# A decode step with new places for its small pieces, and a second quarter of the chosen rows loaded by SyncE

## What is computed

```python
rows_full = concat([cache_kv[page_table], rows_new])     # 4096 + 1 rows a request, from pages
kc, vc = compress(rows_full[:, :, 0]), compress(rows_full[:, :, 1])   # 255 compressed rows
o_cmp, p = cmp_attention(q, kc, vc)
sel = top_k(select_blocks(p), 16)                       # 16 blocks of 64 rows, for each group
o_slc = selected_attention(q, blocks(rows_full[:, :, 2]), blocks(rows_full[:, :, 3]), sel)
o_win = window_attention(q, last 512 rows)
o = g0 * o_cmp + g1 * o_slc + g2 * o_win
```

## Time and profile before

| | |
|---|---|
| median of three runs | 2114.49 us (2113.04 to 2121.23) |
| the profiled execution | 2107.58 us, its span 2105.8 us |
| TensorE busy | 1971.9 us (94% of the span) |
| VectorE, ScalarE, GpSimd busy | 882.5, 735.3, 565.1 us |
| mean granted TensorE clock | 0.983 |

### The profile page before, as it was taken

One profiled execution on the slowest core, in us unless ns is written; L12 is line 12 of the kernel. 1 busy time (PEld: TensorE's weight loads), 2 busy tenths in 40 slices (PEclk: granted clock), 3 DMA queues, 4 the chain that ended last, 5 costly groups with the idle time before them and its releaser, 6 DMA issues. The chain is left out here.

```text
span 2105.8 us, 25188 instructions
## 1 busy us (share of the span) xinstructions
PE 1971.9 (94%) x9303; PEld 1356.8 (64%) x9303; DVE 882.5 (42%) x1781; ACT 735.3 (35%) x1345; POOL 565.1 (27%) x585
## 2 busy tenths in 40 slices
PE   8999999999999999999996898888888888899997
PEld 7888888888888887777774454444444444444442
DVE  0354545454531014444445355454554545511127
ACT  0231133213310003223323665666566665510013
POOL 0000000000002003343345476656466565030000
PEclk9999999999999999999998999999999999999999
DMA  5222222222222321111114555547374563563224
GB/s 199 89 80 91 91 71 80 91 91 71 80 82 102 100 95 48 61 41 41 41 41 140 170 160 171 168 156 218 107 211 143 176 214 111 196 241 142 80 80 161
DMA packets 76486, 248.95 MB, mean 118 GB/s; under 512 B 11764, under 2 KB 35520, under 8 KB 62176
## 3 DMA queue, kind: packets, MB, share of 16 engines
q1 hardware_dynamic: 46312, 148.04, 20.4%
q0 software_dynamic: 28800, 95.45, 15.0%
q10 hardware_dynamic: 1280, 4.23, 0.5%
HBM read 225.17 MB, written 22.49 MB: 118 GB/s over the span
## 5 line engine op out<-in xcount | busy, mean ns | idle before, releaser
L292 PE MATMUL pj<-xT,strips 128*128 128x260 f32 x2368 | 533.2, 384 | 6.3 <-DMA xT<-d_xT 6.3
L292 PEld LDWEIGHTS pj<-xT,strips 128*128 128x128 f32 x2368 | 446.4, 191 | 72.3 <-issue 6.2
L1869 ACT ACTIVATE big<-dtb 64x512 f32<-64x512 f32 x512 | 302.9, 592 | 164.0 <-PE dtb L1601 152.3
L792 PE MATMUL pj<-xT,strips 128*128 128x260 f32 x1216 | 291.0, 387 | 0.0
L1624 PE MATMUL dpH<-big,w 128*128 128x512 f32 x512 | 274.3, 621 | 0.9 <-DVE hs L1992 0.9
L792 PEld LDWEIGHTS pj<-xT,strips 128*128 128x128 f32 x1216 | 222.0, 190 | 59.1 <-issue 29.6
L1975 DVE TENSOR_TENSOR big<-big 128x512 f32<-128x512 f32 x128 | 88.1, 689 | 217.9 <-ACT big L1869 217.9
L1018 POOL MEMSET kbd<- 128x128 f32 x1 | 0.2, 204 | 635.9 <-POOLq L126 635.9
L1044 POOL TENSOR_SCALAR old<-old,rd 128x128 f32<-128x128 f32 (+3 forms) x116 | 122.0, 1066 | 166.8 <-DVE rd L1153 166.8
L1601 PEld LDWEIGHTS dtb<-const,xT 128*128 128x128 f32 x512 | 66.3, 150 | 127.8 <-issue 86.9
L1567 POOL DMA_INDIRECT KV<-d_cache,gi x104 | 102.4, 985 | 169.4 <-DVE gi L2111 140.1
(11 more groups left out here) (312 smaller groups left out, 2345.4 us busy)
## 6 DMA issues: line engine op xcount, KB each, us to landing
strips<-d_w_in SPq DMA_DIRECT2D x60, 1024.0 KB, 5.1
xT<-d_w_out SPq DMA_DIRECT2D x16, 1024.0 KB, 7.7
d_win_sample<-Wt SPq DMA_DIRECT2D x8, 1024.0 KB, 7.3
Xr<-d_w_out SPq DMA_DIRECT2D x8, 1024.0 KB, 8.6
Wt<-d_win SPq DMA_DIRECT2D x8, 896.0 KB
oT<-d_cache SPq DMA_DIRECT2D x84, 80.0 KB
xT<-d_xT SPq DMA_DIRECT2D x8, 520.0 KB, 9.8
Sold<-d_state SPq DMA_DIRECT2D x8, 512.0 KB, 5.2
```

What stands on the lines that cost most here:

```text
L292: mm = nc.tensor.matmul(pj[b][:, a, 0:TH], w[b][:, k, :], xT[:, k, a * TH:(a + 1) * TH], start=(k == 0), stop=(k == KT - 1))
L792: mm = nc.tensor.matmul(bank(s)[:, n, 0:TH], w[s % 2][:, k, :], xT[:, k, n * TH:(n + 1) * TH], start=(k == 0), stop=(k == KT - 1))
L1869: ins = A(dst[:, :, :, hd], tb[bank][hd * DH:(hd + 1) * DH].rearrange("p (j h n) -> p j h n", j=2, h=2), ACT.Copy)
```

## The change

Three things. The table `AT` gets new numbers for some twenty pieces; `LAST` stays. `LOADS` becomes (1, 3): SyncE loads the second quarter as well, 16 loads of 64 rows a request, where GpSimd made eight gathers of 128 rows. And at the start GpSimd issues the gathers of the first quarter of page rows ahead of its four memsets.

```diff
         AT = {
-            "queries": 19, ("second", 0): 27, ("second", 1): 29, "scores": 31, "weights": 35, "sums": 37,
...
+            "queries": 19, ("second", 0): 26, ("second", 1): 29, "scores": 31, "weights": 35, "sums": 37,
...
-        LOADS, GATHERS = (3,), [1 + KVH, 2 * KVH, 2 * KVH, 3 * KVH]
+        LOADS, GATHERS = (1, 3), [1 + KVH, 4 * KVH, 2 * KVH, 3 * KVH]
...
         def _(pool):
...
-            for n in range(2):
-                nc.gpsimd.memset(qbd[n][:], 0.0).then_inc(init, 1)
-            nc.gpsimd.memset(pn[:], 0.0).then_inc(init, 1)
-            nc.gpsimd.memset(sc[:], FORCED).then_inc(init, 1)
...
-            for q in range(4):
+            rows(0, 0, 0)
+            for n in range(2):
+                nc.gpsimd.memset(qbd[n][:], 0.0).then_inc(init, 1)
+            nc.gpsimd.memset(pn[:], 0.0).then_inc(init, 1)
+            nc.gpsimd.memset(sc[:], FORCED).then_inc(init, 1)
+            for q in range(1, 4):
                 rows(0, q, 0)
```

More of the change, by code:

```diff
@@ L1340, in decode_output_phase @@
         AT = {
-            "queries": 19, ("second", 0): 27, ("second", 1): 29, "scores": 31, "weights": 35, "sums": 37,
[L1342 to L1346, removed]
+            "queries": 19, ("second", 0): 26, ("second", 1): 29, "scores": 31, "weights": 35, "sums": 37,
+            "first": 38, "values": 41, "slots": 42, "bases": 43, "turned": 46, "rows": 48,
+            ("second", 2): 53, "fetch0": 54, ("second", 3): 56, "keys0": 57, "mix": 59, "fetch1": 61, "acc": 62,
+            "keys1": 63, "fetch2": 73, "keys2": 75, "fetch3": 78, "keys3": 81,
+            "SCORES": 87, "SCALE": 92, "NEWEST0": 93, "NEWEST1": 99, "TURNED": 100, "VALUES": 103,
+            "WSCORES": 106, "WSCALE": 108, "WTURNED": 112, "WVALUES": 114, "SUM": 117, "DONE": 124,
         }
```

## The result

The changed kernel takes **2062.86 us** (median of four runs, 2061.39 to 2063.73) against 2113.76 us (four runs) for the kernel before: ratio 0.9752, 95% interval 0.9728 to 0.9777, so 2.5% faster. The profiled execution is one of 2063.33 us, 44.25 less than that of before; the sum forecast -43.2.

What follows compares the result with a forecast made beforehand. TensorE was taken to set the pace, idling 12.8 of 88.8 us a request behind short VectorE and ScalarE steps. Terms summed to -43.2 us: 2064.4 profiled, 2071 as median; forecast 2058 to 2086 (0.62), 8 in 10 within 2050 to 2098.

Steps and rivals of the forecast that it cites:

- Slots 39 to 66: `turned` to `TURNED`, then `keys0` to `WTURNED`: waits go, -3.4 us seven times and -2.6 us six times.
- Slots 66 to 78: `SUM`, `DONE`, `second`: `SUM` delays `join_sum`, 4.45 us of waiting against 3.45; +0.3 us, six times.
- Slots 78 to 87: `fetch3`, `keys3`: the 1.3 us wait for ScalarE's copy goes; -0.9 us, seven times.
- New waits: TensorE waits 1.4 us at slot 43, behind the exponential, and about 2 us at slot 48, for the bank of `turned`.
- rivals 1 and 2: Waits return at full size (2097 us, chance 0.17) or no change (0.06); sign: low clock behind slot 48 in every request.
- The start: Memsets behind the first gathers win some 0.7 us; 1.0 more for the first request's `turned`; -1.7 us together.
- The loads: SyncE's sixteen loads take 19.5 us a request, 8.7 to spare: cost nothing; GpSimd's eight fewer gathers worth nothing.
- The end: Last request's quarter 1 loads land behind x, 30.6 us after its issue, so `keys1` waits: +2.4 us once.
- The waits at full size: Chains at slot 48 and slots 72 to 77 each 2 us longer, costing 26 us: 2097 us, chance 0.17.
- no change: Lower clock also falls on the new 2 us wait and both chains lengthen: 2107 to 2120 us, chance 0.06.
- Slower by SyncE: SyncE's sixteen loads land after the place of `fetch1`, slower at 2.24 us a load: about 2130 us, chance 0.05.
- More than expected: New waits at slots 48 and 72 hidden, full clock returns everywhere: 2045 us, chance 0.10.

Runs made afterwards that it cites:

- e2: Changed kernel with the last request's `second` 3 one unit earlier, ahead of VectorE's first addition of x: 2155.53 us, 0.938 of the kernel before on that chip.
- e3: e2 with GpSimd gathering quarter 1 of the last request instead of SyncE loading it: 2147.96 us, 0.935 of the kernel before on that chip.
- e8: e2 with the register of each quarter 1 load read three times instead of once: 2255.60 us, 0.980 of the kernel before on that chip.
- e9: The kernel before, unchanged, profiled on a fourth chip: 2299.18 us, ratio 1.000.
- e11: The kernel before with its old table, SyncE also loading quarter 1: 2180.07 us, 0.948 of the kernel before on that chip.

## Why the prediction was right

**The pace of the requests.** Of the forecast -45.6 us up to the first output product, the trace shows -50.3 (1839.17 to 1788.87). By parts, from the products L1704 of successive requests:

| part | forecast | measured |
|---|---|---|
| start, to the first L1704 | -0.7 | +0.9 |
| first request | -1.9 | -0.6 |
| six requests | -39.6 | -47.3 |
| slots behind the last L1704 | -3.4 | -3.3 |

Within one request, five steps that have kept their slots can be set against each other, `SCORES` (slot 39), the first `join_sum`, `mix` (59), the middle `join_sum` and `scores` (79). Before:

```profile
1383.90 1.78 PE L1683 MATMUL dpS<-KgT,qbd 128*8 128x512 f32 x8
...
1398.84 0.67 DVE L1992 TENSOR_TENSOR hs<-dpH,hs 128x512 f32<-128x512 f32 x1
...
1425.00 1.04 PE L1712 MATMUL dpK<-vc,PTcd 128*16 128x256 f32 x4
...
1459.17 0.60 PE L1683 MATMUL dpK<-kcT,qbd 128*8 128x255 f32 x4
```

and after:

```profile
1457.63 1.79 PE L1683 MATMUL dpS<-KgT,qbd 128*8 128x512 f32 x8
...
1472.39 0.67 DVE L1992 TENSOR_TENSOR hs<-dpH,hs 128x512 f32<-128x512 f32 x1
...
1493.23 1.04 PE L1712 MATMUL dpK<-vc,PTcd 128*16 128x256 f32 x4
...
1512.14 1.27 DVE L1992 TENSOR_TENSOR hs<-dpH,hs 128x512 f32<-128x512 f32 x2
...
1526.07 0.60 PE L1683 MATMUL dpK<-kcT,qbd 128*8 128x255 f32 x4
```

The steps are 14.94, 26.16, 19.42 (to 1444.42) and 14.75 us before, and 14.76, 20.84, 18.91 and 13.93 after.

The first `join_sum` comes no earlier, as the prediction said: VectorE's and ScalarE's chain sets that stretch. The gain is behind it, where before 3.34 us of waiting and the low clock lay. To set the terms against the trace, the products (L1624) can be counted, two rows a slot; this is the time between the products of two slots, as a mean of the second to the seventh request:

| slots | forecast | measured |
|---|---|---|
| 39 to 66 | -6.0 | -7.3 |
| 66 to 78 | +0.3 | +1.1 |
| 78 to 87 | -0.9 | -1.7 |

Some work has crossed slot 66 (`WVALUES`), so the first two are best read together: -6.2 where -5.7 was forecast.

- *Slots 39 to 66*: -7.9 in the three requests in which the clock stays full behind slot 48, -6.4 to -7.4 in the other three.
- *Slots 66 to 78*: the time grew, as forecast, but the waiting did not. TensorE's waits are 3.0 us, where 4.45 had been worked out and 3.45 stood before. The wait at `join_sum` is 1.22 us as worked out (1.3), but those behind it are smaller: the two turns 0.65 and 0.32 (1.1 and 0.65 forecast), the copy L2015 0.82 (1.4):

```profile
1512.95 1.10 PE L1624 MATMUL dpH<-big,w 128*128 128x512 f32 x2 [1.22 <-DVE hs L1992]
1514.70 0.66 PE L1601 MATMUL dtb<-const,Xr 128*128 128x128 f32 x4 [0.65 <-ACT big L1869]
1516.54 0.66 PE L1601 MATMUL dtb<-const,Xr 128*128 128x128 f32 x4 [0.32 <-ACT big L1869]
1522.69 0.65 PE L1672 MATMUL dpK<-hs,w2v 128*64 128x256 f32 x4 [0.82 <-DVE kcT L2015]
```

  They stand in series behind one late step; the likely reason is that each had been sized as if the one ahead of it had not already moved TensorE back. No run tests that.
- *Slots 78 to 87*: -1.1 measured in four of the six requests (as `scores` to L1704 above, 10.11 to 8.98). In the other two it is -2.8, because before the wait for `keys3` had been followed by a stretch of half clock that is gone. No term of the forecast held that: 3.4 of the 7.7 us by which the six requests did better.
- *New waits*: 1.26 us at slot 43 (1.4) and 1.36 at slot 48 (about 2), as here:

```profile
1465.18 0.63 PE L1601 MATMUL dtb<-const,Xr 128*128 128x128 f32 x4 [1.26 <-ACT big L1869]
1473.34 0.66 PE L1601 MATMUL dtb<-const,xT 128*128 128x128 f32 x4 [1.35 <-DVEq L2060]
```

  In the first request the one at slot 48 is 3.10 where it had been 1.92 us, and a stretch of low clock follows; the forecast had a gain of 1.0 there.
- *The low clock.* Six of the seven stands ahead of `TURNED` (3.34 us) had a granted clock of half speed beside or behind them, the last one (2.82 us) had not. In the decode slots ten such stretches (51 us) have become seven (38 us). Four of the seven follow the new wait at slot 48; rivals 1 and 2 would have shown one in every request.

The sum is better than its parts, and that is luck. By its own count the prediction left 9 to 10 us of waiting in a request; 6.0 are left (81.60 less 75.59 in the window above). The waiting fell by 6.8 us a request instead of 3 to 4, and all that the prediction had put beside the waits, the return of the full clock among it, brought some 1 us instead of 3.

**The start.** The forecast -0.7 for the memsets is 0: the wait is 13.6 us against 13.7. The memsets took 0.5 us ahead of the first gather, but that gather starts only 0.1 us earlier against TensorE than before. The +0.9 of the table lies ahead of the change: the whole phase begins 0.8 us later.

**The loads.** In the steady requests they cost nothing on the first chip, and their price was right: sixteen in 19.6 us (19.5 forecast), and no wait for `oT<-d_cache` but one of 0.2 us, on VectorE in the first request.

```profile
1468.31 19.59 SPq L1481 DMA_DIRECT2D oT<-d_cache  x16
```

**The end.** +2.4 was forecast, +6.0 came. The step that failed is the one not taken: the prediction followed the last request's `keys1` into the output projection, and not `second` 3, whose one slot is two units there and leads past the addition that waits for x. The time worked out for the loads (30.6 us after x's issue) is the one measured (31.0), but by luck: x came after 23.4 us and not 27.3, with twelve gathers beside it where there had been twenty, and the loads took 7.5 us more behind it and not 3.3, at 227 GB/s in that stretch and not 385. The wait that belongs to them lay behind the stall at `mix`; e2 and e3 show both, one behind the other. That the loads stand behind x agrees with the Trainium skill ("DMA: Bandwidth & Descriptors", Queues, rings and completion order: a DMA engine takes the descriptors of a queue in ring order): x is used 23.4 us after its issue, the loads 31.0 after it, and when they are taken away (e3), the wait at `keys1` falls from 3.90 to 0.82 us.

The errors nearly cancel, again by luck: -4.7 in the slots, +3.6 at the end. The median lies 8 us under the forecast mainly because the prediction added 6.9 us for the distance between the profiled execution of before and its median; the profiled execution of after lies 0.5 from its own median.

**The rivals.** The waits at full size and no change are excluded by the rows above. Slower by SyncE is excluded for loads of 1.22 us. e8 shows that its mechanism is there for loads of 2.6 us, though even then the kernel is 2% faster than before on its chip. More than expected needed 19 us more than the sum (2045 against 2064.4); the slots gave 4.7.

## What to carry to other kernels

When a table that is counted in one unit is unrolled into a place that is counted in another, follow every moved piece to its last instance there: one slot was two units, and led past an instruction that waits for a transfer. A step that is queued behind a wait for DMA inherits that wait, and so does whoever kept his place and needs it. Waits behind one late step are better sized in series than each from the old schedule (here 3.0 us came of 4.45); and removing one of two waits in series shows its worth only when the other is gone too.

## What the runs showed of the hardware

Three of four chips ran the same kernel 9% slower (2299 against 2114 us), and nearly all of it in the decode slots: a request took 112 to 117 us instead of 88 to 90, while the first L1704 came at 1226.4 instead of 1217.1 us. The program is the same. In the decode slots of e9 TensorE waits 239 us instead of 106, and it is busy 639 instead of 588, since it was granted half clock (1.2 of 2.4 GHz) for 225 us there and for 51 on the first chip. One thing that differs is how long small instructions take. These are SyncE's register operations for its loads, first in the changed kernel on the first chip, then in e11 (count: shortest/median/longest in ns):

```profile
L1481 SPq FUSED_REGOPS  x224: 51/51/56, 1229.9 to 1840.5; - x112
```

```profile
L1481 SPq FUSED_REGOPS  x224: 2/51/1487, 1237.5 to 1962.8; - x112
```

Now and then one takes up to 1.5 us instead of 0.05: in e11 17 of the 224 take over 0.1 us, and 16 of these begin while GpSimd is gathering, where a third of all begin. In e9 the twelve loads of the last request, which come after the last gather, are undisturbed (the second row), and those of the requests before, beside GpSimd's gathers, are not (the first):

```profile
L1481 SPq MOVE oT<-d_cache x84: 3/29/782, 1280.0 to 1981.6; - x84
...
L1481 SPq MOVE w<-d_cache x12: 29/29/38, 2062.4 to 2076.5; - x12
```

A gather itself takes 949 ns as a median there and 946 on the first chip. So where SyncE's small instructions are held up on these chips, GpSimd is nearly always gathering; that ScalarE's gaps have the same cause is a guess, for the reasons given with e9. What it is on those chips that does this stays open: no run varied the gathers alone with the rest of the kernel unchanged, and the trace has no record of its cause. Its weight is plain: of the 185 us that the kernel before lost there, 119 came back by giving eight gathers a request to SyncE (2299 to 2180 us), an edit that nothing in the first chip's trace would have asked for.
